# A transformer pair on one core: mLSTM head order, a gate bank and unread products in the forgetting attention

## The reference, cut to what matters

```
proj = h @ w_in[l]
x_m, o_pre, i_fw, f_fw, i_bw, f_bw, a_q, a_k, a_v = jnp.split(proj, split_points, axis=-1)
i_f, logf_f = gate(i_fw, b_igate[0]), jax.nn.log_sigmoid(gate(f_fw, b_fgate[0]))
```

```
w_intra = jnp.exp(D - m_t[..., None]) * jnp.einsum('bhcte,bhcje->bhctj', q, k)
num = w_inter[..., None] * jnp.einsum('bhcte,bhced->bhctd', q, C_prev) + jnp.einsum('bhctj,bhcjd->bhctd', w_intra, v)
h = num / jnp.maximum(jnp.abs(den), jnp.exp(-m_t))[..., None]
```

```
s = jnp.einsum('bihd,bjhd->bhij', qb, kf)
s = s + cb[..., :, None] - c[..., None, :]
p = jax.nn.softmax(s, axis=-1)
return jnp.einsum('bhij,bjhd->bihd', p, vf)
```

## Time and profile before

| what | us |
|---|---|
| median of 3 runs (lowest, highest) | 2920.34 (2919.67, 2921.5) |
| the profiled execution: its own time | 2914.89 |
| its span, first to last instruction | 2913.1 |
| PE busy, share of the span | 2682.3, 92% |
| DVE, ACT, POOL busy | 951.2, 683.5, 229.2 |

### The profile page before, as it was taken

The page is one execution under the profiler, slowest core; times in us unless marked ns, Lnnn a source line. Parts: engine busy times, 40 slices in busy tenths (PEclk is TensorE's granted clock), DMA queues, the critical chain, the costliest instruction groups (busy, mean ns, idle before and its releaser), DMA issues.

```text
span 2913.1 us, 36568 instructions
## 1 busy us (share of the span) xinstructions
PE 2682.3 (92%) x15700; PEld 1914.0 (66%) x15700; DVE 951.2 (33%) x1506; ACT 683.5 (23%) x1165; POOL 229.2 (8%) x234
## 2 busy tenths in 40 slices
PE   6998687999999999999799889999999988999998
PEld 4755573444444444444588668999999775788886
DVE  4656522121111111111532535333234253433323
ACT  3326420111001001101331333222222133322222
POOL 2434100000000000000200600000000060000000
PEclk9999887999999999999899889999999887999998
DMA  7280035999999999999420112333231020233321
GB/s 264 100 301 26 30 146 208 417 427 427 427 427 425 427 425 428 427 425 426 123 74 22 58 30 60 91 89 102 70 98 60 29 66 15 73 92 89 101 81 57
DMA packets 238511, 558.33 MB, mean 192 GB/s; under 512 B 29537, under 2 KB 191715, under 8 KB 213436
## 3 DMA queue, kind: packets, MB, share of 16 engines
q1 hardware_dynamic: 234160, 548.48, 49.0%
q0 software_dynamic: 1488, 5.70, 0.6%
q10 hardware_dynamic: 2748, 2.47, 0.3%
HBM read 552.39 MB, written 4.23 MB: 191 GB/s over the span
## 4 chain that ended last, share of the span: by engine, by line
PE 83%; DVE 6%; ACT 3%; issue 1%; DVEq 0%; POOL 0%; ACTq 0%
PE vpsum L2210 20%; PE vpsum L2074 15%; PE apsum L2210 11%; PE vpsum L2091 8%; PE apsum L2058 4%; PE apsum L2219 3%; PE apsum L2236 2%; PE vpsum L2236 2%; PE vpsum L2121 1%; PE apsum L2121 1%; PE apsum L2140 1%; PE vpsum L2351 1%; PE apsum L2302 1%; PE apsum L2389 1%; PE vpsum L1992 1%
## 5 line engine op out<-in xcount | busy, mean ns | idle before, releaser
L2074 PE MATMUL vpsum<-ring,arena 128*64 128x512 f32 x2048 | 448.9, 596 | 0.8 <-ACT arena L1010 0.8
L2210 PE MATMUL vpsum<-work_r,wring_r 128*128 128x264 f32 (+1 forms) x2160 | 344.6, 321 | 3.3 <-DVE work_r L1698 3.3
L2210 PE MATMUL apsum<-stream_r,wring_r 128*128 128x264 f32 (+1 forms) x2208 | 337.2, 313 | 0.0
L2210 PEld LDWEIGHTS vpsum<-work_r,wring_r 128*128 128x128 f32 x2160 | 310.7, 188 | 37.5 <-issue 5.9
L2074 PEld LDWEIGHTS vpsum<-ring,arena 128*64 128x64 f32 x2048 | 144.8, 137 | 282.6 <-issue 282.3
L2210 PEld LDWEIGHTS apsum<-stream_r,wring_r 128*128 128x128 f32 x2208 | 309.3, 193 | 22.2 <-issue 1.2
L1602 DVE TENSOR_TENSOR wring_r<-wring,wring_r 128x2048 fp32r<-128x2048 f32 (+2 forms) x97 | 200.3, 2069 | 351.4 <-ACT wring_r L1063 351.4
L2210 PE MATMUL vpsum<-stream_r,wring_r 128*128 128x264 f32 (+1 forms) x1728 | 272.9, 317 | 10.5 <-DVE body L1685 10.5
L1063 ACT ACTIVATE wring_r<-wring 128x2048 fp32r<-128x2048 f32 (+3 forms) x100 | 172.6, 1728 | 467.6 <-DMA wring<-w_ffn 449.9
L2210 PEld LDWEIGHTS vpsum<-stream_r,wring_r 128*128 128x128 f32 x1728 | 246.2, 191 | 31.8 <-DVE body L1685 10.9
L2091 PE MATMUL vpsum<-ring,arena 128*64 128x512 f32 x1024 | 226.8, 595 | 11.0 <-ACT arena L1024 11.0
(11 more groups left out here) (427 smaller groups left out, 3049.3 us busy)
## 6 DMA issues: line engine op xcount, KB each, us to landing
ring<-w_gate SPq DMA_DIRECT2D x64, 2048.0 KB, 17.1
ring<-w_up SPq DMA_DIRECT2D x64, 2048.0 KB, 10.1
ring<-w_down SPq DMA_DIRECT2D x64, 2048.0 KB, 13.7
wring<-w_ffn SPq DMA_DIRECT2D x88, 512.0 KB, 4.7
ring<-w_ada SPq DMA_DIRECT2D x12, 2048.0 KB, 14.9
wring<-w_ffn SPq DMA_DIRECT2D x32, 704.0 KB, 4.4
ring<-w_in SPq DMA_DIRECT2D x5, 2048.0 KB, 19.2
wring<-w_in SPq DMA_DIRECT2D x10, 1024.0 KB, 5.4
```

What stands on the lines that cost most here:

```text
L2074: last = pe.matmul(banks[g][CAP * blk:CAP * blk + CAP, :], xin[:, 2 * r + c, :], w[:, at:at + 512], start=r + c == 0, stop=r + c == 4)
L2210: last = pe.matmul(dst, w_[:, c, col:col + P], x_.bitcast(FR), start=c == 0 and i == 0, stop=c == chunks - 1 and i == 2)
```

## The change

Five edits.

1. The gate product goes to a bank of the A ring (stage `gates` of plan A, right after `ms1`). The stages `gates` and `gates_even` leave plan V, so the four banks of the query projection follow right on the modulation's. DVE reads the gates at the same place in its list, and now frees an A bank.
2. In the mLSTM, rows, scores and weights of head h+1 stand ahead of the sums of head h, on PE and on DVE. For the last head nothing is left to go ahead.
3. W has a second buffer for odd heads. Its two parts lie in memory that the attention's weights and the query and key block matrices have left by then.
4. In fox, after each of the steps except each pair's first query tile (i == 0), PE makes three fp32r products of 128 by 512 into abank[3], which nobody reads; before them it waits until the last heads in that bank were taken out. That makes 12 such groups in a layer, 72 products in all.
5. `mix_low` of the five chunks stands no longer ahead of the fox steps but one in each of the steps 1 to 5, after the step's normalization.

```diff
--- before.py
+++ after.py
@@ -156,15 +156,15 @@
         km = region(R3 + 4096, MH * S, "p (c t) -> p c t", c=MH)
         vm = region(R3 + 6144, TT * MH * 129, "p (t h d) -> p t h d", t=TT, h=MH)
         wbd = [region(at, MH * P, "p (h d) -> p h d", h=MH) for at in (R3 + 8208, R3 + 8720)]
-        W = region(R3 + 9744, 2 * 1280, "p (d x) -> p d x", d=2)
+        W = [[region(at, 1280, "p x -> p x") for at in pair] for pair in ((R3 + 9744, R3 + 11024), (R3 + 12304, R3 + 8208))]
         E = region(R3, 2 * 2 * S, "p (a d t) -> p a d t", a=2, d=2)
         assert R3 + 14864 <= R5 + 1024 <= ARENA
 
-        def Wt(d, jt):
+        def Wt(h, d, jt):
 
             start, width = (sum(S - P * j for j in range(jt)), S - P * jt) if d == 0 else \
                            (sum(P * (j + 1) for j in range(jt)), P * (jt + 1))
-            return W[:, d, start:start + width]
+            return W[h % 2][d][:, start:start + width]
 
 
         shared = sb("shared", [P, 2176])
@@ -234,11 +234,11 @@
         MOD_ROW_AT = {0: 11, 3: 8, 4: 9, 6: 10}
         MOD_PREV = {11: 7, 8: 11, 9: 8, 10: 9}
 
-        V = Plan([("xT", KC), ("colsA", 1)] + first_mods() + [("gates", 1), ("gates_even", 1), ("aqT", 4), ("akT", 4), ("colsA2", 1), ("colsB", 1), ("bvec", 3),
+        V = Plan([("xT", KC), ("colsA", 1)] + first_mods() + [("aqT", 4), ("akT", 4), ("colsA2", 1), ("colsB", 1), ("bvec", 3),
                   ("xm", MH)] + mod_stages(4, 8) + [("gcol", 2)] + list(attention_stages())
-                 + [("vm", TT)] + [st for h in range(MH) for st in [(f"score{h}", TT), (f"hout{h}", 2 * TT)]]
+                 + [("vm", TT)] + [("score0", TT)] + [st for h in range(MH) for st in [(f"score{h + 1}", TT), (f"hout{h}", 2 * TT)] if st[0] != f"score{MH}"]
                  + [("ymT", MH), ("mix", KC), ("route", TT), ("affE", 1), ("rankE", 1)])
-        A = Plan([("ms1p", 1), ("ms1", 1)] + [st for t in range(TT) for st in [(f"av{t}", 1), (f"ss{t}", 1)]] + [(f"ss{c}", 1) for c in range(4, 8)]
+        A = Plan([("ms1p", 1), ("ms1", 1), ("gates", 1)] + [st for t in range(TT) for st in [(f"av{t}", 1), (f"ss{t}", 1)]] + [(f"ss{c}", 1) for c in range(4, 8)]
                  + [("sigo", MH), ("qkm", 2 * MH)] + [(f"rows{h}", 2) for h in range(MH)]
                  + [("ms2p", 1), ("ms2", 1), ("h2tok", 2 * TT)])
 
@@ -880,7 +880,7 @@
                 act.wait_ge(h_done, c + 1)
                 act.activation(f_hi[:, c, :].bitcast(FR), hT[:, c, :], ACT.Copy).then_inc(h_high, 1)
             input_high(K_W)
-            act.wait_ge(v_freed, V.count("gates_even"))
+            act.wait_ge(a_freed, A.count("gates"))
             tmp = gates[0:40, 2, :]
             act.activation(tmp, gates[0:40, 1, :], ACT.Abs).then_inc(act_step, 1)
             act.wait_ge(act_step, 1)
@@ -1293,14 +1293,11 @@
             for c in range(KC):
                 stream_low(c)
             dve.wait_ge(gate_in, 16 * 4)
-            b = take("gates")
+            b = A.take(dve, abank, a_filled, "gates", 0)
             dve.tensor_scalar(gates[0:40, 0, :], b[0:40, :], bgate[:, 0:1], None, ALU.add).then_inc(gate_out, 1)
             dve.tensor_copy(gates[0:40, 1, :], b[GATE_AT[1]:GATE_AT[1] + 40, :]).then_inc(gate_out, 1)
             dve.wait_ge(gate_out, 2)
-            dve.tensor_scalar(gates[0:40, 1, :], gates[0:40, 1, :], bgate[:, 1:2], None, ALU.add).then_inc(v_freed, 1)
-            dve.wait_ge(v_freed, V.count("gates"))
-            take("gates_even")
-            dve.nop().then_inc(v_freed, 1)
+            dve.tensor_scalar(gates[0:40, 1, :], gates[0:40, 1, :], bgate[:, 1:2], None, ALU.add).then_inc(a_freed, 1)
             dve.wait_ge(x_stored, 16)
             for c in range(4):
                 dve.tensor_copy(aq[:, c, ::-1], take("aqT", c)[:, :]).then_inc(v_freed, 1)
@@ -1423,15 +1420,20 @@
             heads_out(PAIRS - 1)
             for t in range(TT):
                 dve.tensor_copy(vm[:, t, :, 0:MD], take("vm", t)[:, :].rearrange("p (h d) -> p h d", h=MH)).then_inc(v_freed, 1)
-            for h in range(MH):
+            def weighted(h):
                 for jt in range(TT):
                     u = h * TT + jt
                     b = take(f"score{h}", jt)
                     for d in range(2):
                         dve.wait_ge(factor_cut, 2 * u + d + 1)
                         lo, hi = (jt * P, S) if d == 0 else (0, jt * P + P)
-                        dve.tensor_tensor(Wt(d, jt), b[:, lo:hi], E[:, u % 2, d, lo:hi], ALU.mult)\
+                        dve.tensor_tensor(Wt(h, d, jt), b[:, lo:hi], E[:, u % 2, d, lo:hi], ALU.mult)\
                            .then_inc(weight_done if d == 0 else v_freed, 1)
+
+            weighted(0)
+            for h in range(MH):
+                if h + 1 < MH:
+                    weighted(h + 1)
                 for t in range(TT):
                     hn = htok[:, t, h * P:h * P + P]
                     assert V.first[f"hout{h}"] % 2 == 0
@@ -1688,8 +1690,7 @@
                 for i in range(3):
                     dve.scalar_tensor_tensor(mixT[:, i, :], flat(take("rt", i))[:, 0:L2], colsL[:, GN + i:GN + i + 1], sgr[:, i, :],
                                              ALU.mult, ALU.mult).then_inc(v_freed, 1)
-                for c in range(5):
-                    mix_low(c)
+
                 def heads_out(pr):
 
                     dve.wait_ge(m_high, MIXES * l + 5 + 2 * pr + 1)
@@ -1713,6 +1714,8 @@
                         link2(dve.reciprocal(ast[0:n, at, 3:4], ast[0:n, at, 2:3]))
                         x = flog[0:n, u % 2, e, 0:w]
                         dve.tensor_scalar(x, x, ast[0:n, at, 3:4], None, ALU.mult).then_inc(fnorm_done, 1)
+                    if 1 <= u <= 5:
+                        mix_low(u - 1)
                     if u >= FU + 1 and i == 0:
                         heads_out(pr - 1)
                 heads_out(FP - 1)
@@ -1862,14 +1865,12 @@
 
             stream = (f_hi, f_lo)
             pe.wait_ge(wgate_done, 8)
-            b = vclaim("gates")
+            b = aclaim("gates")
             for c in range(KC):
                 pe.wait_ge(h_done, c + 1)
                 pe.matmul(b[0:GATE_W, :], wgate[:, c, :], hT[:, c, :], start=c == 0, stop=c == KC - 1).then_inc(h_used, 1)
             pe.wait_ge(h_used, KC)
-            pe.nop().then_inc(v_filled, 1)
-            vclaim("gates_even")
-            pe.nop().then_inc(v_filled, 1)
+            pe.nop().then_inc(a_filled, 1)
             w = inputs(Q_W)
             dense_by_chunk([vclaim("aqT", m) for m in range(4)], w, stream, v_filled, lambda c: pe.wait_ge(h_low1, c + 1), range(KC))
             w = inputs(K_W)
@@ -1967,7 +1968,7 @@
             for m in range(2 * MH):
                 pe.wait_ge(xc_done, m % MH + 1)
                 pe.matmul(aclaim("qkm", m)[:, :], wbd[m // MH][:, m % MH, :], xc[m % MH], start=True, stop=True).then_inc(a_filled, 1)
-            for h in range(MH):
+            def memory_scores(h):
 
                 for d in range(2):
                     b = aclaim(f"rows{h}", d)
@@ -1978,6 +1979,11 @@
                     if jt == 0:
                         pe.wait_ge(a_freed, A.count("qkm"))
                     pe.matmul(b[:, :], km[:, h, jt * P:jt * P + P], qm[:, h, :], start=True, stop=True).then_inc(v_filled, 1)
+
+            memory_scores(0)
+            for h in range(MH):
+                if h + 1 < MH:
+                    memory_scores(h + 1)
                 for t in range(TT):
                     for d in range(2):
                         b = vclaim(f"hout{h}", 2 * t + d)
@@ -1989,7 +1995,7 @@
                             pe.wait_ge(v_freed, V.count(f"score{h}", max(tiles)))
                         for jt in tiles:
                             at = (t - jt if d == 0 else t) * P
-                            last = pe.matmul(b[:, 0:MD + 1], Wt(d, jt)[:, at:at + P], vm[:, jt, h, :],
+                            last = pe.matmul(b[:, 0:MD + 1], Wt(h, d, jt)[:, at:at + P], vm[:, jt, h, :],
                                              start=jt == tiles[0], stop=jt == tiles[-1])
                         last.then_inc(v_filled, 1)
             for h in range(MH):
@@ -2393,6 +2399,16 @@
                             last = pe.matmul(dst[64 * e:64 * e + 64, :], vf[0:META, TT, hv], metaT[e][0:META, x0:x1], start=x0 == S, stop=True)
                         last.then_inc(fo_filled if x0 == 0 else turnM_filled, 1)
 
+                def keep_clock(pr, i):
+
+                    drained = FP * l + pr - (i == TT)
+                    if i == 0:
+                        return
+                    if drained >= 1:
+                        pe.wait_ge(fo_freed, drained)
+                    for c in range(3):
+                        pe.matmul(abank[3][:, :], ident_r[:].bitcast(FR), h_hi[:, c, 0:S].bitcast(FR), start=True, stop=True)
+
                 pe.wait_ge(v_freed, VLl.count("negc"))
                 pe.wait_ge(a_freed, ALl.count("pm"))
                 pe.wait_ge(mask_done, 2)
```

1 line of the change is left out of this document (added).

## The result

The changed kernel takes **2885.2 us** (2884.5 to 2885.9, 4 runs) against 2920.0 (2918.6 to 2921.5, 4 runs) of the kernel before: ratio 0.9879, 95% interval 0.9867 to 0.9891. That is 34.8 us faster. Forecast were 2899 with a range of 2889 to 2910: the sign was right, the gain was 14 us larger and lies outside the range. Run once more later, beside other kernels, it took 2885.5 (2883.7 to 2887.3).

A forecast was written before the change was run, and what follows sets the result against it. PE was 83% of the chain, held or slow at the gate product, mLSTM heads and fox; the expert stage, bound by weights, only moves. -9.7 - 10.5 - 3 + 2 = -21.2 us gave 2893.7 profiled, 2899 median; range 2889 to 2910.

The forecast's parts named there:

- The gate bank: Gate product: PE's wait before the first query product shrinks by 8.15 us, full clock adds 1.6; together 9.7 us gained.
- early gain lost: Rival: a transfer or POOL's cutting holds a projection, only 2 of 9.7 us remain, 2907; chance 0.09.
- The mLSTM heads: mLSTM heads: overlapping one head's sums with the next head's work gains 11.0 us, counted as 10.5; bounds 7 to 12.5.
- the period: mLSTM heads: time from one head's weights to the next's, claimed to fall from 14.4 to 13.1 us.
- the ring: mLSTM heads: closed cycle of sums, rows, factors and weights that sets a head's period: 3.75 + 0.1 + 1.07 + 8.16 us.
- The end: mLSTM heads: after the last weights DVE has two heads of sums, eight steps of 1.36, 10.9 us.
- The unread products: Fox: regained clock gives 4.5 us, products cost 3; net -1.5 in a layer, -3 in both.
- my first rival: Fox: the clock is regained nearly everywhere, products' term -8 in a layer, 2886; chance 0.13.
- The moved low parts: Fox: moving them costs DVE +1.0 us in a layer, +2 in both; bounds -1.8 to +2.5 in a layer.
- the term by the rule: Fox low parts: by the skill's rule on DVE and POOL blocking, 0 instead of +2, and the sum 2897.
- the step from the profiled execution to the median: Whole kernel: the median of the runs shown lies 5.4 us above the profiled execution; carried over, 2893.7 becomes 2899.

The follow-up runs named there:

- The second run of after: The changed kernel itself, unchanged source, run once more beside other kernels: 2885.5 us.
- the warmer kernels: The changed kernel with more unread products in other waits of PE, in several variants: 2859.4, 2862.8, 2869.3 and 2867.6 us.
- after with products ahead of the queries: The changed kernel plus 16 unread 128x128 products in the wait ahead of fox's query projections: 2888.0 us.
- low parts as before: The changed kernel with the five low parts in one block ahead of fox again, unread products kept: 2894.3 us.
- the first set of experiments: Against the changed kernel: without products 2906.1, low parts back in their block 2894.3, both 2905.8 us; the kernel before with the products alone 2906.6.
- the two kernels that have 75.5 and 76.3: The kernel before with the gate bank edit alone, 2914.3 us; the changed kernel without unread products and with low parts in their block, 2905.8.

## Why the prediction was wrong, point by point

**The gate bank.** Right where it is made. The first query product was forecast at 48.2 and is at 48.36, the projection at 21.8 us and takes 21.84, the key projection 9.7 earlier and is 9.5. By the rows of head 0 it is 10.2. Alone, however, it is worth 6.7 us and not 9.7. Between the profiles it is fox that takes time back, 5.7 us; for the medians the place isn't shown. The rival "early gain lost" was right in kind only for the kernel that has this edit alone, and no projection lost the gain.

**The mLSTM heads.** 8.7 instead of 10.5 us. The first half of the forecast holds: ACT goes from head 0 to head 1 without a gap, the gaps later are 7.31 and 6.95 us instead of 9.00 and were forecast near 6. The failed part is the period, forecast 13.1, measured 14.4 and 14.0. PE's timeline from the last weight of head 1 to the rows of head 2, answering to the earlier trace rows:

```profile
284.34 5.08 PE L1998 MATMUL vpsum<-arena 128*128 128x129 f32 x26 [0.57 <-DVE arena L1430]
289.35 1.98 PE L1976 MATMUL apsum<-arena,ident 40*128 40x512 f32 x4
```

DVE's timeline beside it, answering to the earlier trace rows:

```profile
283.59 0.69 DVE L1430 TENSOR_TENSOR arena<-vpsum,arena 128x512 f32<-128x512 f32 x1 [0.71 <-POOL arena L734]
...
286.14 0.16 DVE L1444 SCALAR_TENSOR_TENSOR den<-vpsum,shared 128x2 f32<-128x2 f32 x1 [0.62 <-PE vpsum L1998]
...
288.29 0.16 DVE L1444 SCALAR_TENSOR_TENSOR den<-vpsum,shared 128x2 f32<-128x2 f32 x1 [0.82 <-PE vpsum L1998]
```

The weights end at 284.28 and the rows start at 289.35, 5.07 later, where I had 3.75 and 0.1. DVE waits 0.62 and 0.82 us for the next pair of banks between its sums, and PE, which fills them, is busy without a gap at a clock of 0.60:

```profile
284.34:289.35 5.01, 5.01 (x26) 4.89 (x26) 3.15 (x15) 0.00 (x0) 0.00 (x0) 0.60 0.00 0
```

The second run of after has the same 26 records behind the weights of head 2 at the full clock. They take 3.59 us, DVE's sums then stand 1.36 apart without a wait, and the rows of head 3 start at 301.67, 3.58 behind the last weight at 298.09:

```profile
298.15 3.59 PE L1998 MATMUL vpsum<-arena 128*128 128x129 f32 x26 [1.09 <-DVE arena L1430]
298.15:301.70 3.55, 3.55 (x27) 3.16 (x27) 3.06 (x14) 0.00 (x0) 0.00 (x0) 1.00 0.02 5
```

That period is 12.9 us. So the ring was drawn rightly; its step for PE was sized at the full clock (4.98/19 = 0.26 a product), while PE fell to the lower level in the waits for the weights, and the 0.5 us that I took off for it was too little. The end is right: eight sum steps behind the last weights take 11.0 us (10.9 forecast).

**The unread products: the step that failed.** The prediction said "No row shows how much comes back; I take half, and three quarters of that on the path: 4.5". This term failed, by its two factors: how much of the half-clock time comes back, and what it is worth. With the whole kernels it can be measured directly: the products bring 13.9 us in the kernel before, 11.5 with the gate bank and the heads and 20.9 with all other edits, where I had 3. In after, of 40.9 us at half clock 30.3 came back in each layer, not 20. And their worth was sized too low. I had 0.87 x 0.33 x 0.75 = 0.22 us for each us at half clock. The 0.33 came from a misread row: I took the 3.05 us of the value products for the full clock, but the clock in that row is a mixture:

```profile
1713.62:1716.60 2.98, 2.98 (x16) 1.35 (x17) 0.00 (x0) 0.00 (x0) 0.00 (x0) 0.76 0.00 0
```

At the full clock they take 2.38 us (below), so the share is 1 - 2.38/4.53 = 0.47, and by my own working 0.31 for each us. What it was worth can be estimated from the windows. The stretches with 36 products and moved low parts, those of the warmer kernels included, lie between 10.6 us at half clock and 66.5 of length, and 27.6 and 72.5: 6.0 us for 17.0, 0.35 us for each us at half clock (without products, from 40.9 and 73.0 to 55.1 and 78.8, it is 0.41; between the first and 51.9 and 76.3 it is 0.30). So the clock gave 30.3 x 0.35 = 10.6 in a layer, an estimate. The cost comes out near the forecast: carried back to no half clock, fox is 66.5 - 3.7 = 62.8 with products and 73.0 - 14.3 = 58.7 without, 4.1 us for 36 products (3 was forecast; with 0.30 or 0.41 for the price it is 2.6 or 5.9). Fox went down by 6.5 us in a layer, where I had -1.5 for the products and +1 for the low parts. In the kernel with the products alone its windows are 3.9 and 3.6 us shorter. This is near my first rival, "the clock is regained nearly everywhere in fox", at 2886, which had 0.13. I had held against it that the steps with values end in products of 16 rows and a wait; but their 16 records (eight products) now take this (PE in fox, answering to the earlier trace rows):

```profile
1650.74 0.97 PE L2410 MATMUL apsum<-stream_r,ident_r 128*128 128x512 f32 x3
...
1653.15 2.38 PE L2395 MATMUL apsum<-body 128*64 128x512 f32 x16 [0.64 <-ACT body L1153]
```

2.38 us, at the full clock, against 4.53 and 3.05. The Trainium skill ("TensorE: Matmul & The Clock Gate", section "Terms") counts as the penalty one half of the time at half clock; by it the gain would be 15.1 us, an estimate. The windows give less, 10.6; that PE waits in a part of that time would fit.

**The moved low parts.** Forecast +1 in a layer. The gain of 1.8 at the start is there: the first reduction comes 3.3 us after fox's start in after, 5.1 in the kernel with the block. At nearly equal time at half clock (after with products ahead of the queries 68.0 and 69.8, low parts as before 69.1 and 69.6) the move is worth -1.1 and +0.3, so about -0.4: inside my bounds, but with the other sign than the value I took. What the whole kernels show beyond that, 9.1 us with the products and none without, is in the first set of experiments; I had no term by which the two edits act on each other. DVE's rows in fox, answering to the earlier trace rows:

```profile
1638.16 1.79 DVE L1629 TENSOR_TENSOR work_r<-body,work_r 128x528 fp32r<-128x528 f32 x1
...
1641.97 0.70 DVE L1629 TENSOR_TENSOR work_r<-body,work_r 128x528 fp32r<-128x528 f32 x1
```

Only the first low part meets POOL and takes 1.79; the next already takes 0.70, where I had reckoned 1.7 for two. (The 0.69 us that I had compared with the block is of an operation with one input in PSUM; this 0.70 is the like one.) POOL's last row in fox is:

```profile
1634.43 4.95 POOL L818 TENSOR_TENSOR wring_r<-wring,wring_r 128x512 fp32r<-128x512 f32 x4
```

POOL ends 10.1 us after fox's start, where it was busy for 12.1 us before. The Trainium skill's rule that the prediction cited ("SBUF — State Buffer", section "Who interferes with whom") agrees with that: with reductions in the place of the block POOL was done 2 us earlier, and the term by the rule, 0, was nearer than mine. Beside POOL some normalizations of DVE are longer too, 1.12 us instead of 0.30 for the same shape, and I had counted nothing for them.

**The balance.** On the profiled scale the forecast was -21.2 and the trace shows -30.6. Fox gave 13.1 instead of 1.0 (12.1 more), the gate bank 0.5 more, the heads 1.8 less; 1.8 of the early gain is gone by the start of fox, and 0.4 came elsewhere. The rest of the 14 us is the step from the profiled execution to the median: I carried over the 5.4 us by which the profiled execution of before lies under its median, and that of after lies only 0.7 under. The runs of before span 2916.0 to 2926.6 in all, eight of after 2883.7 to 2887.3. Those of before go with the clock: over the whole span it is 0.946 in the profiled run of before, 0.943 or 0.944 in the runs near the median, and 0.942 in the slowest, at 2926.6. Whether that lower clock lies in fox is not shown.

## What to carry to other kernels

A stretch where TensorE alternates between small products and short waits at a granted clock between 0.5 and 1 has a price of its own, which can be read: 2 x (1 - clock) x length, times about a third here. Take the worth of the full clock from a row whose own window shows 1.00. Unread full-array products in its waits buy it back here, and the right number is found by trying two or three counts, since beyond it they cost most of their time and narrow ones only cost. Before crediting an early gain in full, look whether a later stretch with a mixed clock keeps its length. And where an edit acts through the clock, measure it with and without the other edits: here their worths did not add up.

## What the runs showed of the hardware

- The same instructions of fox took 73.0, 75.5 and 76.3 us at granted clocks of 0.72, 0.68 and 0.66; the two kernels that have 75.5 and 76.3 repeat both numbers to 0.04 us although one starts fox 7.9 us before the other.
- The same 16 records of the modulation take 1.92 us in one run and 3.64 in another, at 1.00 and 0.50, with nothing changed ahead of them; the first query product stands at 48.4 or 51.1 to 51.3 us with it.
- Products on 16 rows and 16 columns stream as many columns as full ones, but left the clock at 0.58, where full ones brought it to 0.92.
- The 32 gather products of 64 columns (64 records) take 13.89 us at half clock and 7.33 at the full one. Under the router's 32 products of 16 columns the clock fell from 1.00 to 0.50 although they were entered at the full one.
- The 13 products of the heads' sums (26 records of 129 columns) take 5.08 us where the clock is 0.60 and 3.59 where it is 1.00.
